# The first norm of a decoder block, taken from an input in transposed layout with sums of squares by products with ones

## The reference

```python
def rms_norm(x, w):
    xf = x.astype(jnp.float32)
    y = xf * lax.rsqrt(jnp.mean(xf * xf, axis=-1, keepdims=True) + RMS_EPS)
    return (y * w.astype(jnp.float32)).astype(x.dtype)
...
...
h = h + hybrid_mixer(rms_norm(h, norm_mix_w[l]), w_in[l], conv_w[l], mu_shift[l], ...)
...
p = xn @ w_in
c_b, c_c, c_h, p_rwkv = jnp.split(p, [CONV_WIDTH, 2 * CONV_WIDTH, 3 * CONV_WIDTH], axis=-1)
```

## Time and profile before

| | us |
|---|---|
| median of 3 runs | 2392.6 |
| lowest, highest | 2390.9, 2393.35 |
| span of the profiled execution | 2391.4 |
| TensorE busy in it | 2313.6 (97%) |
| VectorE, ScalarE, GpSimd busy | 818.7, 454.8, 328.0 |
| chain that ended last, TensorE's share | 90% |

### The profile page before, as it was taken

How to read it: one execution, slowest core, us unless ns; L and a number is a source line. 1 busy time by engine, 2 the same in 40 slices (tenths; PEclk the granted TensorE clock), 3 DMA queues, 4 the chain that set the end, 5 groups by cost and what they waited for, 6 DMA issues and landing times.

```text
span 2391.4 us, 47109 instructions
## 1 busy us (share of the span) xinstructions
PE 2313.6 (97%) x18686; PEld 1716.3 (72%) x18687; DVE 818.7 (34%) x1941; ACT 454.8 (19%) x920; POOL 328.0 (14%) x342
## 2 busy tenths in 40 slices
PE   7999999799989989999999999999999999999997
PEld 4443444688854577788788878887888788778875
DVE  2466511466653332222222222222222222222224
ACT  3322100122332311111111111111111111111113
POOL 0000000011101231121121112111111121112112
PEclk9999999899999989999999999999999999999999
DMA  3011110311152277688878787788798789868977
GB/s 122 32 69 35 53 53 35 129 44 46 41 224 91 87 278 258 262 333 309 307 297 297 309 317 287 279 304 339 269 338 309 291 309 344 308 247 311 345 306 253
DMA packets 101355, 530.02 MB, mean 222 GB/s; under 512 B 25939, under 2 KB 50663, under 8 KB 76704
## 3 DMA queue, kind: packets, MB, share of 16 engines
q1 hardware_dynamic: 79152, 484.45, 51.9%
q0 software_dynamic: 22160, 44.98, 7.4%
HBM read 485.24 MB, written 40.05 MB: 220 GB/s over the span
## 4 chain that ended last, share of the span: by engine, by line
PE 90%; DVE 4%; DMA 2%; issue 2%; ACT 1%; POOL 0%; SPq 0%; POOLq 0%; DVEq 0%; ACTq 0%
PE ps L1707 37%; PE ps L1727 18%; PE ps L1356 13%; PE ps L1619 5%; PE ps L1737 2%; PE ps L1716 2%; PE ps L1529 2%; PE ps L1503 2%; PE ps L1525 1%; PE ps L1746 1%; DMA arena<-arena 1%; DVE arena L1028 1%; PE ps L1387 1%; PE ps L1468 1%; DMA idx_g<-list_s 1%
## 5 line engine op out<-in xcount | busy, mean ns | idle before, releaser
L1707 PEld LDWEIGHTS ps<-arena 128*128 128x128 f32 x7808 | 925.8, 191 | 16.1 <-issue 14.8
L1707 PE MATMUL ps<-arena 128*128 128x128 f32 (+2 forms) x7808 | 926.6, 281 | 1.1 <-ACT arena L873 1.1
L1727 PE MATMUL ps<-arena 128*128 128x512 f32 x1024 | 453.7, 596 | 0.0
L1356 PE MATMUL ps<-arena 128*128 128x512 f32 x832 | 361.8, 594 | 0.8 <-ACT arena L715 0.8
L1727 PEld LDWEIGHTS ps<-arena 128*128 128x128 f32 x1024 | 190.4, 190 | 221.5 <-issue 220.7
L1253 DVE TENSOR_SCALAR arena<-ps,arena 128x160 f32<-128x160 f32 x256 | 98.3, 384 | 614.8 <-PE ps L1707 534.2
L1356 PEld LDWEIGHTS ps<-arena 128*128 128x128 f32 x832 | 157.6, 190 | 202.4 <-issue 202.4
L878 ACT ACTIVATE arena<-arena 128x160 f32<-128x160 f32 x256 | 86.4, 337 | 824.3 <-DVE arena L1253 824.3
L618 POOL DMA_INDIRECT sum_s<-arena,idx_s x31 | 51.6, 1663 | 823.3 <-ACT arena L893 823.3
L1619 PE MATMUL ps<-arena 128*128 128x512 f32 x256 | 112.8, 595 | 2.1 <-DVE arena L1155 2.1
L1257 DVE SCALAR_TENSOR_TENSOR arena<-arena 128x160 f32<-128x160 f32 x256 | 83.4, 326 | 50.0 <-ACT arena L878 50.0
(11 more groups left out here) (261 smaller groups left out, 1898.3 us busy)
## 6 DMA issues: line engine op xcount, KB each, us to landing
arena<-gu_w SPq DMA_DIRECT2D x128, 2048.0 KB, 13.3
arena<-dn_w SPq DMA_DIRECT2D x64, 2048.0 KB, 14.0
arena<-dn_b SPq DMA_DIRECT2D x32, 512.0 KB, 16.2
arena<-w_in_t SPq DMA_DIRECT2D x26, 512.0 KB, 3.3
arena<-arena SPq DMA_DIRECT2D x32, 256.0 KB, 2.7
arena<-x SPq DMA_DIRECT2D x4, 1024.0 KB, 8.4
arena<-w_out SPq DMA_DIRECT2D x2, 2048.0 KB, 13.0
arena<-x SPq DMA_DIRECT2D x8, 512.0 KB, 6.1
```

Of the source, the lines that this page charges most:

```text
L1356: last = nc.tensor.matmul(ps[:, bank + h, :], win[:, slot, kt * P:(kt + 1) * P], xnT[:, kt, h * HALF:(h + 1) * HALF], start=kt == 0, stop= ...
L1707: last = nc.tensor.matmul(ps[:, f % 2, k * C:k * C + size], wslot[u][:, kt, o:o + P], xT[:, kt, 0:size], start=kt == 0, stop=kt == KT - 1, ...
L1727: last = nc.tensor.matmul(ps[:, 2 + h, :], actT[:, ft, 0:P], wslot[4 + h][:, ft, :], start=ft == 0, stop=ft == KT - 1)
```

## The change

Beside `x` the kernel gets the same numbers in transposed layout, `xT`, as 8 slabs of 128 features by 1024 tokens, and reads the slabs in place of the rows for the first norm (the later residual still reads rows of `x`). ScalarE squares a slab. The sum over features is now a sum over partitions, so TensorE makes it: four products with a matrix of ones, each for 256 tokens, each into its own 32 rows of PSUM bank 3, accumulated over the 8 slabs. ScalarE takes the root of (sum/1024 + epsilon) in one instruction on 128 x 256 elements, VectorE the reciprocal on the same. Four products of one row of ones with one row of the reciprocals spread it over all 128 rows, 256 tokens each. VectorE multiplies each slab by weight and reciprocal root, 512 tokens at a time, into `xnT`. The diagonal matrices, the 64 transposing products and ScalarE's 32 evacuations are gone.

```diff
+        xraw = at(0, KT, T)
+        squares = [at(32 + 4 * k, T) for k in range(2)]
+        SPAN = T // 4
+        rs_q = at(40, SPAN)
+        rows1 = sb("ones_rows", [P, P])
...
         def _(sp):
-            for g in range(4):
-                sp.dma_start(xs[:, 2 * g:2 * g + 2, :], x[2 * g * P:2 * (g + 1) * P, :].rearrange("(t p) n -> p t n", p=P)
-                             ).then_inc(s_x[g], 16)
-                if g == 0:
+            for k in range(KT):
+                sp.dma_start(xraw[:, k, :], xT_d[k]).then_inc(s_x[k // 2] if k < KT - 1 else s_xl, 16)
+                if k == 0:
                     sp.dma_start(cst[:, :], consts_d[:, 0:K_MIX]).then_inc(s_par, 16)
                     sp.dma_start(prm[:, :], prm_d).then_inc(s_par, 16)
...
         def _(act):
+            for k in range(KT):
+                act.wait_ge(*((s_x[k // 2], 32) if k < KT - 2 else (s_x[k // 2], 16) if k < KT - 1 else (s_xl, 16)))
+                if k >= 2:
+                    act.wait_ge(s_ms, k - 1)
+                nc.scalar.activation(squares[k % 2], xraw[:, k, :], ACT.Square).then_inc(s_sq, 1)
+            act.wait_ge(s_ms, KT)
+            act.wait_ge(s_rq, 1)
+            nc.scalar.activation(rs_q, ps[:, 3, 0:SPAN], ACT.Sqrt, scale=1.0 / D, bias=rmseps[:, :]).then_inc(s_rt, 1)
...
         def _(dve):
+            nc.vector.memset(rmseps[:, :], RMS_EPS)
+            nc.vector.memset(rows1[:, :], 1.0).then_inc(s_rq, 1)
+            dve.wait_ge(s_rt, 1)
+            nc.vector.reciprocal(rs_q, rs_q).then_inc(s_rq, 1)
             dve.wait_ge(s_par, 2 * 16)
+            for h in range(2):
+                dve.wait_ge(s_rb, 2 * h + 2)
+                for k in range(KT):
+                    w = slice(h * HALF, (h + 1) * HALF)
+                    nc.vector.scalar_tensor_tensor(
+                        out=xnT[:, k, w].rearrange("p (b t) -> p b t", t=SPAN),
+                        in0=xraw[:, k, w].rearrange("p (b t) -> p b t", t=SPAN), scalar=prm[:, NWM + k:NWM + k + 1],
+                        in1=ps[:, 4 + 2 * h:6 + 2 * h, 0:SPAN], op0=ALU.mult, op1=ALU.mult).then_inc(s_xn, 1)
...
         def _(pe):
+            def square_sums(k):
+                pe.wait_ge(s_sq, k + 1)
+                for g in range(4):
+                    last = nc.tensor.matmul(ps[32 * g:32 * (g + 1), 3, 0:SPAN], rows1[:, 0:32],
+                                            squares[k % 2][:, g * SPAN:(g + 1) * SPAN], start=k == 0, stop=k == KT - 1,
+                                            skip_group_check=True)
+                last.then_inc(s_ms, 1)
+
+            pe.wait_ge(s_rq, 1)
+            for k in range(KT):
+                square_sums(k)
+            pe.wait_ge(s_rq, 2)
+            for g in range(4):
+                nc.tensor.matmul(ps[:, 4 + g, 0:SPAN], rows1[32 * g:32 * g + 1, :], rs_q[32 * g:32 * g + 1, :],
+                                 start=True, stop=True).then_inc(s_rb, 1)
+
+            def early_half(n, h):
+                if h == 0:
+                    pe.wait_ge(s_w[n], 16)
+                for kt in range(KT):
+                    if n == 0:
+                        pe.wait_ge(s_xn, KT * h + kt + 1)
+                    last = nc.tensor.matmul(ps[:, ring_pair(n) + h, :], win[:, n, kt * P:(kt + 1) * P],
+                                            xnT[:, kt, h * HALF:(h + 1) * HALF], start=kt == 0, stop=kt == KT - 1)
+                last.then_inc(s_pj, 1)
+
+            for h in range(2):
+                early_half(0, h)
+                early_half(1, h)
             pe.wait_ge(s_pi, 16)
```

More of the change, by code:

```diff
@@ L113, in link, with build @@
         self.eng.wait_ge(self.sem, self.base + self.n)
-def build(nc, x, w_in_t, prm_d, lora_d, wgate_d, normw_d, w_out, router_w, router_b, gub_d, gu_w, dn_w,
+def build(nc, x, xT_d, w_in_t, prm_d, lora_d, wgate_d, normw_d, w_out, router_w, router_b, gub_d, gu_w, dn_w,
           dn_b, consts_d, list0_d, entry_d, out, conv_d, bonus_d, xn_d, acc_d, list_d):
@@ L148, in build @@
         ones2 = cst[:, K_ONES2:K_ONES2 + P]
-        xs = at(0, TT, D)
-        sqj = at(32, D)
-        diag = [at(36 + 0.5 * k, P) for k in range(2)]
+        xraw = at(0, KT, T)
[3 more added lines that the diff above has]
+        rows1 = sb("ones_rows", [P, P])
         AR = at(0, RT, NCH, 2, L)
@@ L215, in build @@
         gneps = sb("gneps", [P, 1])
+        rmseps = sb("rmseps", [P, 1])
         spare = sb("spare", [P, 1])
@@ L261, in build @@
         s_sq = sem("squares")
-        s_ms = sem("mean_square")
+        s_xl = sem("x_last_in")
+        s_ms = sem("square_sums")
         s_rt = sem("root")
+        s_rq = sem("ones_then_reciprocal_root")
+        s_rb = sem("root_on_all_rows")
         s_xn = sem("x_normalised")
-        s_tr = sem("x_transposed")
-        s_te = sem("xT_evacuated_act")
-        s_tv = sem("xT_evacuated_dve")
         s_w = [sem(f"w_in{k}") for k in range(3)]
@@ L897, in square_sum @@
             def square_sum(t, loads, before):
-                act.wait_ge(s_x[t // GROUP], 16 * loads)
+                act.wait_ge(s_x[t // GROUP], 16 * (loads + (t // GROUP < GROUPS - 1)))
                 act.wait_ge(s_sq2, before)
@@ L944, in _ @@
             ch = Chain(dve, s_dv)
[L945 to L953, removed]
-            dve.wait_ge(s_par, 2 * 16)
[L956 to L971, removed]
+            nc.vector.memset(rmseps[:, :], RMS_EPS)
+            nc.vector.memset(rows1[:, :], 1.0).then_inc(s_rq, 1)
+            dve.wait_ge(s_rt, 1)
+            nc.vector.reciprocal(rs_q, rs_q).then_inc(s_rq, 1)
+            dve.wait_ge(s_par, 2 * 16)
+            for h in range(2):
[6 more added lines that the diff above has]
+                        in1=ps[:, 4 + 2 * h:6 + 2 * h, 0:SPAN], op0=ALU.mult, op1=ALU.mult).then_inc(s_xn, 1)
             dve.wait_ge(s_pi, 16)
@@ L1405, in _ @@
+            for h in range(2):
+                early_half(0, h)
+                early_half(1, h)
             pe.wait_ge(s_pi, 16)
-            for n in range(2):
-                project(n, ring_pair(n), 1).then_inc(s_pj, 1)
             def norm(i):
@@ L1820 @@
         "x": a["x"][0],
+        "xT": a["x"][0].T.reshape(KT, P, T),
         "w_in_t": w_in_t,
```

## The result

The changed kernel takes 2432.16 us, median of 4 executions (2426.77 to 2440.83), the kernel before in the same comparison 2392.97 us (2390.9 to 2393.37). The ratio is 1.0171, with a 95% interval of 1.0158 to 1.0184. Predicted were 2385.3 us and a range up to 2389.8. The profiled execution has a span of 2434.5 us, 43.1 more than before.

What follows compares the result with a forecast made beforehand. TensorE, busy 97% of the span, was taken as the bound. The new start's steps, with 1.7 us clock loss, put tile n=2 at 50.8 us instead of 58.1, so 2392.6 - 7.3 = 2385.3 us, range 2382.8 to 2389.8.

Steps and rivals of the forecast that it cites:

- the last of the rivals: Scan loop: its moved code is fetched again in each later pass, 7 x 3.5 = 24.5 us added, 2409.8 us; chance 0.08.
- the mark: Input projection: start of tile n=2, the comparison point, at 58.1 us before and forecast at 50.8 us after.
- Last slab and its square: Start, new norm: last slab of x lands at 15.1 us, ScalarE's square of 1.06 us ends at 16.2 us.
- Sums: Start, new norm: TensorE's four products overlap by 1.75, 0.98 us a slab; only the last slab's is late, about 17.3 us.
- The rival of sums one by one: Start, new norm: the four sums do not overlap, 1.72 us a slab, gain only 5.4 us, 2387.2 us; chance 0.19.
- Root: Start, new norm: ScalarE's root on 128 x 256 from PSUM takes 0.47 us, from 17.5 to 18.0 us.
- Reciprocal: Start, new norm: VectorE's reciprocal takes 1.64 us, to 19.6 us, the dearest new step.
- Spreading: Start, new norm: VectorE waits for two products of 256 columns without overlap, 1.0 us with tail, to 20.6 us.
- First operand: Start, before the projection: VectorE's 128 x 512 multiply with a PSUM input takes 0.69 us, to 21.3 us.
- Four halves: Start of the input projection: TensorE does four halves of 6.87 us, 27.5 us, to 49.1 us.
- 1.7 for the clock: Start of the input projection: TensorE's wait lowers the granted clock, costing 1.7 us, to 50.8 us; bound nothing.
- A shift at the mark passes to the end: Behind the start of tile n=2: waits are for counts, so the 7.3 us gained there reaches the kernel's end.

Runs made afterwards that it cites:

- e3: The changed kernel with the scan loop's code placed one slot behind the start of a block of 256 instructions: 2387.06 us, ratio 0.9979 to the kernel before.
- e4: The changed kernel with the scan loop's code placed 130 slots behind the start of a block of 256 instructions: 2396.49 us, ratio 1.0021 to the kernel before.

## Why the prediction was wrong

The step that failed is the last of the rivals, "by my count of instructions the loop lies over eight such blocks before and after, just as many as it holds, so I expect no change", which had got a chance of 0.08. With it fell what the sum rests on behind the mark, that a shift there passes through to the end because every wait is for a count: a stop for code waits for no count. The mechanism was named, its first-pass stops were in the earlier trace rows and its sign was right; I dismissed it by a rule and a count. The Trainium skill (Runtime: NRT & Kernel Launch, Instruction fetch mechanics) gives TensorE's instruction store 2048 instructions, eight blocks, and calls it a FIFO; that a loop over eight blocks therefore stays in it was my inference, which it does not state. The traces refute it: 34 loads of code where the loop lies over seven blocks, 97 where it runs 124 slots into an eighth. And my count of where the loop begins need not start where the blocks do: I had it over eight blocks before and after alike, yet the kernel before fetches one block from its third pass to the output projection and its copy 132 slots on fetches again in five passes, so the loop before lies over seven blocks or hardly reaches an eighth. Its price was too low as well: 24.5 us forecast as seven passes of 3.5, 48.1 measured as six passes of 8.0, since I took the first pass's two stops as a whole pass's price and left out the clock that falls at the stops.

The steps of the sum, point by point:

- **Last slab and its square:** 16.2 us forecast, 17.7 measured. The slabs of one semaphore are taken up in pairs; the pair of slabs 4 and 5 lands at 13.39 us, and four squares of about 1 us and a wait of 0.3 us for the sums follow. I had costed each slab as if it were taken when it landed.
- **Sums:** 0.98 us a slab forecast, 1.12 in the changed kernel and 0.64 for the later slabs of e3. Hidden by the table load, as forecast: line 694's load ends at 19.03 and the root starts at 19.05. The rival of sums one by one (1.72 us) is refuted.
- **Root:** 0.47 us forecast, 0.48 measured. **Reciprocal:** 1.64 and 1.76. **Spreading:** 1.0 and 0.84. The row from which I took that row groups do not overlap, 16 instructions in 1.88 us, stands in a stretch with a granted clock of 0.50 (0.55 from 440 to 442 us); the same 16 take 1.16 us at 505.53, at 1.00. So the reason was wrong, at little cost here. **First operand:** 0.69 and 0.76. The chain from last square to first projection was 5.4 us, as forecast.
- **Four halves:** 27.5 us and 1.7 for the clock forecast, 30.50 measured, so 3.0 for the clock. Its mechanism was right, its size was not. PE and the others around it in the changed kernel:

```profile
19.00:21.00 2.00, 0.00 (x0) 0.00 (x0) 1.45 (x1) 0.51 (x2) 0.00 (x0) 1.00 0.13 51
21.00:23.00 2.00, 0.74 (x8) 0.31 (x8) 1.08 (x3) 0.00 (x0) 0.00 (x0) 0.73 0.00 0
23.00:25.00 2.00, 1.88 (x3) 0.88 (x4) 2.00 (x4) 0.00 (x0) 0.00 (x0) 0.50 0.03 8
25.00:27.00 2.00, 2.00 (x4) 0.97 (x3) 2.00 (x4) 0.00 (x0) 0.00 (x0) 0.50 0.00 0
27.00:29.00 2.00, 2.00 (x4) 0.69 (x4) 2.00 (x4) 0.00 (x0) 0.00 (x0) 0.56 0.00 0
29.00:31.00 2.00, 2.00 (x6) 0.94 (x5) 2.00 (x4) 0.00 (x0) 0.00 (x0) 1.00 0.00 0
```

- **A shift at the mark passes to the end:** right up to the scan (4.5 us at 53.6, 4.1 at 287), and right all the way once the loop is placed: e3 ends 4.5 us of span below the kernel before, 2386.9 against 2391.4.

So 1.5 us for the square and 1.3 for the clock make up the 2.8 us that the start fell short, and the scan's code makes up the rest.

## What to carry to other kernels

An edit that adds or takes instructions ahead of a long loop, here one of some seven code blocks, moves that loop, and can cost more than the edit is worth: look for stops with no releaser in the later passes and compare the count of code loads, then place the loop by a directive, whose padding does not run, and judge the edit only with both kernels placed. When a term is dismissed by a count of a capacity, leave a margin of one unit, and price it by the whole pass. And before a long run of products, shorten the wait and fill what is left of it: idle time there was paid twice, once as itself and once in the clock.

## What was not expected of the hardware

- A program with one and the same order of instructions spread over 41 us (2386.41 to 2427.24) in e4, by how many passes fetched their code again. The changed kernel spread over 14 us, the well placed e3 over 3.4.
- Short instructions that only count up a semaphore cost TensorE about 0.15 us each: with 164 of them its first product is at 26.1 us, with 156 at 25.0, counted from 1 us.
- Products into four groups of 32 output rows run beside each other far better than the halves in the earlier trace rows had shown: 8 instructions of 256 columns in 0.64 us with their tail, where 1.72 us would be one by one, 2.7 times. The Trainium skill (TensorE: Matmul & The Clock Gate, Part 3) gives 2.38 for three groups of 512 columns and has no figure for four; the trace, with one group more, lies above it.
- The profile's clock column reads 1.00 at the start of the kernel while 8 of these instructions take 1.12 us, and still 1.00 when they take 0.64; it shows the fall at 22 us, not the slow beginning. The factor, 1.75, is near the 1.79 between the 2.08 us and the 1.16 us of the scan's 16 instructions at 0.50 and 1.00, which suggests the lower clock there too; no run shows it.
